# Routed-expert outputs weighted on leaving PSUM, with the second picks' rows added to the residual by GpSimd's adding transfers

## The reference

```python
def hier_moe(h, w_rg, b_rg, w_re, b_re, w_gate, w_up, w_down):
    ...
    g_w = jnp.take_along_axis(g_prob, g_idx[:, None], axis=-1)
    ...
    top_v, top_i = lax.top_k(e_in, EXPERT_TOPK)          # two picks a token
    top_p = jax.nn.softmax(top_v, axis=-1)
    ...
    for g in range(N_EXPERT_GROUPS):
        a = jnp.einsum('nd,edf->nef', hf, w_gate[g])
        u = jnp.einsum('nd,edf->nef', hf, w_up[g])
        act = jax.nn.silu(a) * u * combine[:, g, :, None]
        out = out + jnp.einsum('nef,efd->nd', act, w_down[g])
x = x + hier_moe(rmsnorm(x, ffn_norm[l]), ...)
```

## Time and profile before

| | us |
|---|---|
| median of 3 runs | 1303.61 (1303.42 to 1305.01) |
| profiled execution, its own time | 1302.57 |
| its span, first to last instruction | 1300.8 |
| PE busy | 1263.1 (97%) |
| DVE busy | 627.3 (48%) |
| ACT busy | 386.8 (30%) |
| POOL busy | 719.9 (55%) |
| expert steps, first `project` to last `down` matmul | 1012.6 to 1286.1 |
| granted TensorE clock, mean | 0.998 |

### The profile page before, as it was taken

One profiled execution on the slowest core, in us unless ns is written; L12 is line 12 of the kernel. 1 busy time (PEld: TensorE's weight loads), 2 busy tenths in 40 slices (PEclk: granted clock), 3 DMA queues, 4 the chain that ended last, 5 costly groups with the idle time before them and its releaser, 6 DMA issues.

```text
span 1300.8 us, 19002 instructions
## 1 busy us (share of the span) xinstructions
PE 1263.1 (97%) x7442; PEld 914.8 (70%) x7442; DVE 627.3 (48%) x1035; ACT 386.8 (30%) x766; POOL 719.9 (55%) x752
## 2 busy tenths in 40 slices
PE   7999999999999999999999999999999999999997
PEld 7888768787788776888888777888878443333333
DVE  4252361448994484624774578543225432222225
ACT  5211262422332585112213654551004011111111
POOL 6677636576666400766865444566771565555430
PEclk9999999999999999999999999999999999999999
DMA  7623311433133200233321314642278699999965
GB/s 241 185 71 110 97 34 34 148 123 98 66 116 112 98 2 1 75 130 124 103 92 49 99 50 147 253 152 98 79 285 317 240 370 409 408 402 406 401 241 194
DMA packets 86845, 216.54 MB, mean 166 GB/s; under 512 B 24292, under 2 KB 33484, under 8 KB 73188
## 3 DMA queue, kind: packets, MB, share of 16 engines
q1 hardware_dynamic: 63132, 199.36, 41.5%
q0 software_dynamic: 14064, 8.45, 2.2%
q10 hardware_dynamic: 9560, 7.51, 1.9%
HBM read 252.98 MB, written 25.96 MB: 214 GB/s over the span
## 4 chain that ended last, share of the span: by engine, by line
PE 75%; DMA 11%; DVE 5%; ACT 3%; POOL 2%; DVEq 2%; SPq 1%; issue 1%; POOLq 0%; ACTq 0%
PE ps L186 18%; PE ps L187 18%; PE ps L188 18%; DMA w_gu<-w_up 9%; PE ps L1226 7%; PE ps L1241 3%; PE ps L892 2%; POOL w_lo L1305 1%; PE ps L1104 1%; PE ps L1012 1%; PE ps L1020 1%; PE ps L1096 1%; PE ps L1115 1%; DVE pr L2198 1%; ACT pr L1493 1%
## 5 line engine op out<-in xcount | busy, mean ns | idle before, releaser
L1302 POOL CAST w_hi<-stage 128x512 fp32r<-128x512 f32 (+1 forms) x280 | 179.4, 682 | 358.6 <-PE ps L188 348.8
L1305 POOL TENSOR_TENSOR w_lo<-stage,w_hi 128x512 fp32r<-128x512 f32 (+1 forms) x280 | 363.2, 1328 | 10.1
L186 PE MATMUL ps<-hi,w_hi 128*128 128x512 f32 (+1 forms) x608 | 237.1, 390 | 1.2 <-DVE lo L1899 0.6
L187 PE MATMUL ps<-hi,w_lo 128*128 128x512 f32 (+1 forms) x608 | 235.3, 387 | 0.0
L188 PE MATMUL ps<-lo,w_hi 128*128 128x512 f32 (+1 forms) x608 | 235.2, 387 | 0.0
L186 PE MATMUL ps<-w_hi,hi 128*128 128x512 f32 (+1 forms) x488 | 176.5, 362 | 1.5 <-POOL w_lo L1305 0.9
L187 PE MATMUL ps<-w_hi,lo 128*128 128x512 f32 (+1 forms) x488 | 174.9, 358 | 0.0
L188 PE MATMUL ps<-w_lo,hi 128*128 128x512 f32 (+1 forms) x488 | 174.8, 358 | 0.0
L1226 PE MATMUL ps<-w_gu,xT 128*64 128x512 f32 x736 | 163.0, 595 | 3.6 <-DMA w_gu<-w_up 3.2
L186 PEld LDWEIGHTS ps<-hi,w_hi 128*128 128x128 f32 x608 | 114.3, 188 | 27.7 <-issue 3.0
L188 PEld LDWEIGHTS ps<-lo,w_hi 128*128 128x128 f32 x608 | 114.2, 188 | 23.2
(11 more groups left out here) (489 smaller groups left out, 1763.7 us busy)
## 6 DMA issues: line engine op xcount, KB each, us to landing
stage<-w_in SPq DMA_DIRECT2D x84, 512.0 KB, 4.5
w_gu<-w_gate SPq DMA_DIRECT2D x32, 1024.0 KB, 13.3
w_gu<-w_up SPq DMA_DIRECT2D x32, 1024.0 KB, 15.9
w_dn<-w_down SPq DMA_DIRECT2D x32, 1024.0 KB, 11.9
stage<-w_out SPq DMA_DIRECT2D x16, 512.0 KB, 4.6
stage<-w_ssd_branch SPq DMA_DIRECT2D x16, 512.0 KB, 4.9
stage<-w_in SPq DMA_DIRECT2D x20, 256.0 KB, 3.1
stage<-w_attn_branch SPq DMA_DIRECT2D x8, 512.0 KB, 4.2
```

Source lines behind the costliest of these rows:

```text
L186: pe.matmul(out, x[0], w[0], start=first, stop=False)
L187: pe.matmul(out, x[1], w[0], start=False, stop=False)
L1302: nc.gpsimd.tensor_copy(hi[:, b, k, 0:n], stage[:, b, k, 0:n])
L1305: last = nc.gpsimd.tensor_tensor(lo[:, b, k, 0:n], stage[:, b, k, 0:n], hi[:, b, k, 0:n].bitcast(F32), ALU.subtract)
```

## The change

Every expert row now takes its share on ACT when it leaves PSUM, so what stands in `y_scratch` is ready to be added. For that `slot_share` has a column for each of the 24 steps, filled by 24 gathers of 4 bytes a slot (`share_of`) where there were two: seven together ahead of the steps, one for step 3, and 16 inside the loop, for step 6 and steps 9 to 23, each at the end of POOL's round s for step s + 4. Those 16 count on `xg_in`, the semaphore of the rows, so `rows_in` grows by 16 for each of these steps. SP writes the shares to HBM in the order of the rows (1024 single elements) and earlier. At the end POOL adds the second picks' 2 MB onto `xres` by four adding transfers, SP reads back only the first picks' 2 MB, and DVE has four additions for eight. `down` of step 23 waits for the two banks one by one.

```diff
 def rows_in(step):
-    return sum(16 if whole(t) else 64 for t in range(step % 3, step + 1, 3))
+    return sum((16 if whole(t) else 64) + (16 if share_with_rows(t) else 0) for t in range(step % 3, step + 1, 3))
...
+def early(step):
+    return not spills(step) and sum(not spills(t) for t in range(step)) < EARLY
+def share_with_rows(step):
+    return not early(step) and step != HALF_STEP
...
             for i in range(2):
                 sp.wait_ge(xg_in[i], 16)
+            sp.wait_ge(rt_step, 3)
+            with nc.allow_non_contiguous_dma(reason="4 KB of shares in the order of the rows"):
+                sp.dma_start(share_dram.rearrange("(a p) o -> p (a o)", p=P), share[:].rearrange("p k t -> p (k t)")).then_inc(share_saved, 16)
             gate_up(5, 5)
...
             for t in range(TT):
-                for k in range(2):
-                    sp.dma_start(back[:, TT * k + t, :], y_dram[S * k + P * t:S * k + P * (t + 1), :]).then_inc(back_in[t], 16)
+                sp.dma_start(back[:, t, :], y_dram[P * t:P * (t + 1), :]).then_inc(back_in[t], 16)
...
+            def share_of(s, signal):
+                q = pair_of(s)
+                nc.gpsimd.indirect_dma_start(slot_share[:, q:q + 1], None, share_dram, bass.IndirectOffsetOnAxis(ap=out_u[:, q:q + 1], axis=0),
+                                             bounds_check=2 * S - 1, oob_is_err=False).then_inc(signal, 16)
...
             gather(2)
+            pool.wait_ge(share_saved, 16)
+            for s in range(STEPS):
+                if early(s):
+                    share_of(s, slots_set)
             pool.wait_ge(over_ready, 1)
...
+                    share_of(HALF_STEP, slots_set)
+                if s + 4 < STEPS and share_with_rows(s + 4):
+                    share_of(s + 4, xg_in[(s + 4) % 3])
+            for s in range(LAST[0] - 3, LAST[0]):
+                pool.wait_ge(y_out[s % 3], 16 * (s // 3 + 1))
+            for t in range(TT):
+                nc.gpsimd.dma_start(xres[:, t, :], y_dram[S + P * t:S + P * (t + 1), :], accum_op=ALU.add).then_inc(added[t // 2], 16)
...
-                A.activation(yg[s % 3][0:p].rearrange("p (c n) -> p c n", c=2), ps[1][0:p, 0:2, :], ACT.Copy).then_inc(y_ready, 1)
+                A.activation(yg[s % 3][0:p].rearrange("p (c n) -> p c n", c=2), ps[1][0:p, 0:2, :], ACT.Copy, scale=slot_share[0:p, q:q + 1])\
+                    .then_inc(y_ready, 1)
...
-            def add_back(t, picks=(0, 1)):
-                V.wait_ge(back_in[t], 32)
-                for k in picks:
-                    V.scalar_tensor_tensor(xres[:, t, :], back[:, TT * k + t, :], share[:, k, t:t + 1], xres[:, t, :], ALU.mult, ALU.add)
-                    V.drain()
+            def add_back(t):
+                V.wait_ge(back_in[t], 16)
+                V.wait_ge(added[t // 2], 32)
+                V.tensor_tensor(xres[:, t, :], back[:, t, :], xres[:, t, :], ALU.add)
+                V.drain()
```

More of the change, by code:

```diff
@@ L40 @@
 HALF_STEP = AHEAD
+EARLY = 7
 LAST = (STEPS - 2, STEPS - 1)
@@ L423, in program @@
         back_in = [sem(f"back_in{t}") for t in range(TT)]
+        added = [sem(f"added{i}") for i in range(2)]
         out_ready = sem("out_ready")
@@ L1864, in high @@
                     A.wait_ge(dn_done, LAST[0] + 2 * j + c + 1)
[L1865 removed]
+                    A.activation(yh[j][:, c], ps[1][:, c, :], ACT.Copy, scale=slot_share[:, q:q + 1]).then_inc(y_ready, 1)
             for s in range(STEPS):
```

60 lines of the change are left out of this document (19 added, 41 removed).

## The result

The changed kernel takes 1323.90 us (median of 6 runs, 1323.21 to 1326.88); the kernel before, run beside it, 1304.31 (6 runs, 1303.25 to 1305.49). The ratio is 1.0149, 95% interval 1.0137 to 1.0161. The forecast was 1312 with a range to 1318: right in sign, 12 us short, outside the range. The profiled execution took 1323.21 us, 20.64 more than that of before.

The account below looks back on a forecast made before the run. It took PE to bound the kernel, with POOL's queue q0 short of turns close behind. The profiled 1302.57 us plus 5.8 (loop shares) and 2.5 (tail) gave 1310.9, the median 1.04 above: 1312, range 1302.5 to 1318.

Parts of the forecast that it names:

- The start: Ahead of step 3's row gather: POOL's 9.7 us wait covers seven share gathers; 0 to 1 us, up to 4, taken 0.
- The shares in the loop: On POOL's queue q0: twelve more small gathers at 0.7 us each make `project(20)` start 5.8 us later; range 0 to 8.3.
- the turn of step 21: On PE before `project(20)`: it waits for step 21's share gather, landing at 1240.6, so `project(20)` starts at 1242.0, 5.8 later.
- POOL's own time: In the loop: three more issues a cycle, 3.9 us, are covered by POOL's idle time; nothing added.
- ACT and small DVE work: Scale operand in an existing ACT instruction, and small DVE instructions dropped in step 3 beside PE; 0.
- The tail: After the steps: four fewer DVE additions, but the third waits for all four adding transfers; 2.0 us earlier to 3.7 later, taken +2.5.
- the upper end, 3.7: In the tail: an adding transfer also reads the residual's rows and counts as two loads; 12 units, 3.7 us later.
- The dear rival: Adding transfers in the tail cost three loads (1318.8), or the start loses 4 us as well (1316); chance 0.13.

Follow-up runs that it names:

- t_low_first: The changed kernel with the share write in contiguous 32-byte pieces and, in DVE's last stage, step 23's two low halves ahead of the third addition; 1310.4 us.
- m_contig_no_loop: The changed kernel with the share write in contiguous 32-byte pieces and without the 16 gathers of shares in the loop; 1315.1 us.

## Why the prediction was wrong, step by step

- **The start (forecast 0 to 1, up to 4; measured 9.96): the step that failed.** I wrote that POOL's wait covers the seven gathers "if the shares are in HBM within 1 to 2 us of their issue", and that was the right condition: at 1.9 us it holds and the start costs 0.0, at 10.3 it fails. I had no row for a write of single elements, took 0 and had 4 us as the worst; no run shows those 4. And I did not follow the failed case to its end: what is then exposed is not the delay of the write but all that hid in the same idle time, the seven gathers (9.1 us) and the place of the row gather ahead of SP's loads.
- **The shares in the loop (forecast 5.8; middle measured 5.24, shares alone 4.4).** The resource was right, POOL's queue; that the number is near is luck. The place was wrong: not the turn of step 21 but DVE's turning, POOL's gathers behind it, and the spill weights of steps 12 to 18; of the spill weights I had only step 21's, and wrote "so I add nothing for the middle". `project(20)` was 5.3 us late beyond the start, 2.8 of it lower clock, for which I had nothing. And the lag did not grow to the end: I had it that "the landing time on q0 doesn't move with PE", with about 30 us for step 21's row gather. It took 8.6 (23.9 before), the last spill transfer for that step 13.8 (20.1 before), and PE turned step 21's rows over without a wait. The 8.2 us of the share gather bring it to 1240.0, nearly the 1240.6 that I forecast, by accident: PE came there only at 1250.98.
- **What I didn't see at all: the share write that leaves SP's queue.** I priced what it adds at its new place and not what it did at its old one, although my first paragraph had it that q0 gets "about one packet for one of q1, whatever its size". It is worth 4 us alone (3.9 by the medians), and hides in the sum because it draws on the same slack.
- **POOL's own time (0): right in the loop.** In the start it was the 9.1 us. **ACT and small DVE work (0):** no run tests it alone, and none speaks against it.
- **The tail (forecast +2.5; measured 4.60).** The mechanism was right, the size off. The unit is 2.7 us by engine time and 3.0 by the landings, at the upper end of my 1.42 to 2.84 or over it, so the upper end, 3.7, was the better value. My reason for going below it, that only one of the two reads comes from HBM, is refuted by the doubled engine time. The Trainium skill ("Collectives: The Full Stack", The bandwidth ceiling) has, for the adding transfers of collectives, two reads for each write and half the rate. By the 39.6% against 19.8% the trace agrees. The remaining 0.9 fits PE, which had to wait for `low` and placed at the lower clock: from the end of the third addition to the end took 8.8 us where I had 7.7. The 3.7 has `low` behind the third addition in it already, so the 0.9 isn't the 2.6 of t_low_first.
- **The range.** The dear rival had "or" between its causes. The start went far beyond its end and the tail past its upper one, and that would have been 1312 + 10 + 2.

Still open: why a wait of some 2 us is sometimes followed by a `project` of 8.78 us and sometimes not (2.88 us in m_contig_no_loop was not, 2.21 was).

## What to carry to other kernels

Idle time that hides work has a condition. Ask what is exposed when it fails: all that hid there, and everything queued behind it. Where the packet counts of two full queues are equal, count packets, also those that an edit takes away: a small transfer on the big queue can be what keeps the small queue in time. And when two edits lean on one resource without slack, undoing one alone shows nothing; run each alone on the kernel before.

## What the runs showed of the hardware

- 1024 single elements of 4 bytes from SBUF to HBM on SP's queue take 10.3 to 11.1 us in the four kernels that have them, and a gather on POOL's queue is late as well (issued at 1013.41 it took 15.7 us to land; one issued at 1010.80, ahead of the write, 2.6). The same 4 KB in 128 pieces of 32 bytes take 1.4 to 2.2 us at that place; behind SP's loads, where the kernel before has them, 17.7.
- Three writes of 128 small packets on SP's queue shortened the landing of a transfer on POOL's, under full load, from 20.1 to 13.4 us.
- An adding transfer of 512 KB from HBM into SBUF takes the DMA engines twice the time of a plain one (39.6% of 27 us for four, against 19.8%).
- A granted clock of 0.81 over one `project` costs 1.7 us; after 6.6 us of idle time PE placed at 0.50 (the window above), after 3.4 us in t_low_first at 1.00.
